# The output projection in token layout: attention output stationary, weights moving in 512 columns

## The chip, the cores and the metric

The kernel runs on one core of a Trainium2 chip. The metric is the device time of one execution in microseconds; lower is better. Times of several executions are given by their median.

## The reference

One layer of an encoder block with 256 tokens and model width 2048, all in float32. What surrounds the change:

```python
mixed = jnp.concatenate([out_a, out_b], axis=-1)   # (1, 256, 2048), the heads' outputs
x = x + mixed @ w_o[l]                             # w_o (2048, 2048): the output projection
h = rms_norm(x, norm_ffn[l])                       # over the 2048 features of a token
x = x + conv_gated_ffn(h, w_up[l], conv_w[l], conv_b[l], w_down[l])   # w_up (2048, 11264), w_down (5632, 2048)
return rms_norm(x, norm_final)
```

Below, y stands for `x + mixed @ w_o`, the residual stream after the projection.

## The kernel before

**Exact float32 by three products.** Every weight tile and every activation is split into a high part (type fp32r) and a low part, the rest. A product is three matmuls into the same PSUM bank: high by high, high by low, low by high (`mm3`, L1002). For each weight tile of 128 x 1024 numbers (512 KB), SP issues the load into a ring of four slots (`raw`), ScalarE writes the high part (`split_hi`, L423), VectorE the low part (`split_lo`, L659), and TensorE multiplies. ScalarE may split tile t once TensorE is through with tile t-4 (`mm_done`), SP may load tile t once the low part of tile t-4 is made (`lo_done`). ScalarE and VectorE run three tiles ahead (`LEAD`). Each engine has one order of work, written out by hand with counting semaphores; nothing is reordered by a planner.

**Stages.** Input projection and attention go in four groups of heads, the attention of one group being laid into the gaps between the tiles of the next. The attention of the last group is laid between the first seven tiles of the output projection (`SLOTS_TAIL`: T transposes probabilities, S makes scores, V multiplies with the values). Then comes the output projection, then the up projection in 22 steps of eight tiles, then the down projection in 88 tiles.

**The output projection before** has 8 units of 256 output features, each of 4 tiles; a tile covers 512 rows of w_o by 256 columns. In `features` (L1008) the weights are stationary and the attention output is moving, in 256 columns (all tokens): 4 row blocks x 2 feature blocks x 3 products = 24 matmuls a tile, 768 in all. The result comes out in feature layout (features on partitions). x, however, lies in token layout in `nat`. So for every unit GpSimd copies 256 columns of x to `xcols` (L403, L406), TensorE transposes them (`turn_x`, L1153, 4 transposes), ScalarE copies them out of PSUM to `xts` (L542), VectorE adds (`make_y`, L831), ScalarE squares (L549) and writes the high part of y times its gain (L551), VectorE adds the squares to `ysum` (L837) and writes the low part (L840). For the later residual y must be in `nat` in token layout as well: TensorE transposes it back (`turn_y`, L1164, 4 transposes) and ScalarE writes it to `nat` (`take_ynat`, L557). The first three units are interleaved by `WOA_ORDER`, units 3 to 7 follow one by one, 4 to 7 in a loop of two passes.

**The second norm's factor** is found behind the first tiles of the up projection: two float32 matmuls with a matrix of ones sum `ysum` over the features and spread the sum over the partitions (L1233), ScalarE takes the root (L594, with a table load), VectorE the reciprocal of 128 x 256 numbers (L878, `r2b`). `r2b` is first used when the first four up tiles are evacuated (L890).

**In the up projection** `up_step` (PE) waits in its first step for the low parts of y that each tile multiplies with; the weights are stationary there, and matmuls of 512 and of 256 columns alternate (L1222, L1224). **In the down projection** (`down`) the activations are stationary and the weights move in 512 columns: 2 row blocks x 2 token blocks x 3 products = 12 matmuls a tile, through the same `mm3`. The result is in token layout and is added to `nat` in place.

Of the kernel before, what the change touches and what calls it, by code (L numbers as in the profile page):

```python
# [5 lines left out]
F32 = mybir.dt.float32  # L25
# [37 lines left out]
T_WOA = T_QUAD + QUADS * QUAD_TILES  # L63
WOA_UNITS = 3
T_WOB = T_WOA + 4 * WOA_UNITS
WO_UNITS = 8
T_UP = T_WOB + 4 * (WO_UNITS - WOA_UNITS)
# [65 lines left out]
def program(nc, x, norm_mix, w_in, sinks, b_f, w_o, norm_ffn, w_up, conv_w, conv_b, w_down, norm_final,  # L133
            ident_c, tri_c, mask_a_c, mask_b_c, cos_c, sin_c, out):
    ctx = ExitStack()
    with ctx:
# [6 lines left out]
        def sem(name):  # L143
# [86 lines left out]
        x_banks = [acc[0][:], acc[2][:], acc[1][:], sc_ps[:, 0], sc_ps[:, 1], tr_ps[:, 0], tr_ps[:, 1], pv_ps[:]]  # L230

# [23 lines left out]
        xcols_s, xt_ps, xts_s, yt_s, ysq_s, yhi_s, ylo_s, yt_ps, ynat_s, ysum_s, y2_ps, y2_root, r2_s = (sem(n) for n in (  # L255
            "xcols_s", "xt_ps", "xts_s", "yt_s", "ysq_s", "yhi_s", "ylo_s", "yt_ps", "ynat_s", "ysum_s", "y2_ps",
            "y2_root", "r2_s"))
# [8 lines left out]
        wo = w_o[0].rearrange("(t c p) n -> t p c n", p=P, c=4)  # L266
# [24 lines left out]
        r3 = small[:, 20:22]  # L291
        g1 = cst[:, 0:KB]
# [10 lines left out]
        def _(sp):  # L303
# [62 lines left out]
        def _(pool):  # L366
# [45 lines left out]
        def _(act):  # L412
# [124 lines left out]
            def take_xt(u):  # L537

                act.wait_ge(xt_ps, u + 1)
                if not (isinstance(u, int) and u == 0):  # L540
                    act.wait_ge(yt_s, u)
                act.activation(xts[:].rearrange("p a n -> p (a n)"), sc_ps[:, 0], ACT.Copy).then_inc(xts_s, 1)  # L542

            def after_y(u, par):

                act.wait_ge(yt_s, u + 1)
                if not (isinstance(u, int) and u == 0):
                    act.wait_ge(ysum_s, u)
                act.activation(ysq[:], yt[:, par], ACT.Square).then_inc(ysq_s, 1)  # L549
                for b in range(2):  # L550
                    act.activation(act_hi[:, bass.ds(u * 2 + b, 1), :].rearrange("p a n -> p (a n)"), yt[:, par, b],  # L551
                                   ACT.Copy, scale=cst[:, bass.ds(u * 2 + (KB + b), 1)]).then_inc(yhi_s, 1)

            def take_ynat(u):

                act.wait_ge(yt_ps, u + 1)
                act.activation(nat[:, :, bass.ds(u * 256, 256)], sc_ps[:, 1].rearrange("p (m n) -> p m n", m=2),  # L557
                               ACT.Copy).then_inc(ynat_s, 1)

            for s in range(4 * WOA_UNITS):  # L560
                split_hi(T_WOA + s + LEAD, (s + LEAD) % RING)
                attention(s, SLOTS_TAIL, QUADS - 1)
                if s in WOA_Y:
                    take_ynat(WOA_Y.index(s))
                if s in WOA_END:
                    after_y(WOA_END.index(s), WOA_END.index(s) % 2)
                if s in WOA_X:
                    take_xt(WOA_X.index(s))

            def wo_unit(u, par):  # L570
                t = u * 4 + (T_WOB - 4 * WOA_UNITS)
                for s in range(4):
                    split_hi(t + (s + LEAD), (s + LEAD) % RING)
                    if s == 0:
                        take_ynat(u - 1)
                    if s == 2:
                        take_xt(u)
                    if s == 3:
                        after_y(u, par)

            wo_unit(WOA_UNITS, WOA_UNITS % 2)
            with act.Fori(0, 2) as i:
                wo_unit(i * 2 + 4, 0)
                wo_unit(i * 2 + 5, 1)
# [725 lines left out]
```

## Time and profile before

| | |
|---|---|
| median of 3 executions | 1118.66 us (1117.6 to 1120.81) |
| span of the profiled execution, first to last instruction | 1116.6 us |
| TensorE matmul busy | 1106.6 us, 99% of the span |
| VectorE busy | 735.4 us, 66% |
| ScalarE busy | 595.8 us, 53% |
| GpSimd busy | 20.9 us, 2% |
| mean granted TensorE clock | 0.998 |
| HBM traffic over the span | 180 GB/s |

The profile gives the profiled execution by its span alone; the median of the timed runs is 2.1 us longer, and that is taken as what lies around the span.

Matmuls are pipelined, so the duration of one in the profile is longer than the time from it to the next: a matmul of 256 columns has 0.28 us, and one starts every 0.12 us. Where time is counted here it goes by starts, or by the number of matmuls in a window of known length. In the chain of waits a group such as "x4" is already in such time. "PE" is matmuls, "PEld" weight loads.

### The profile page before, as it was taken

The page shows a single profiled execution, that of the slowest core. Times are in us where ns is not written, and L with a number is a line of the kernel's source. Part 1 is how long each engine was busy: PE and PEld are TensorE (multiplying, and loading weights), DVE is VectorE, ACT ScalarE, POOL GpSimd, SP SyncE. Part 2 cuts the span into 40 slices and gives each one's busy share as a digit, 9 for nine tenths or more (in the row PEclk, how much of TensorE's full clock was granted, in tenths as well). Part 3 has the DMA queues.
Part 4 walks back from the last instruction along what each step waited for, and adds up shares of the span by engine and source line. Part 5 has one row for each costly group of instructions (what it writes and reads, how often), then busy time and mean ns, then how long its engine had stood idle before and what let it go on. Part 6 is the DMA issues. An engine that isn't in the chain of part 4 may idle for free.

```text
span 1116.6 us, 19616 instructions
## 1 busy us (share of the span) xinstructions
PE 1106.6 (99%) x6873; PEld 978.1 (88%) x6873; DVE 735.4 (66%) x1126; ACT 595.8 (53%) x910; POOL 20.9 (2%) x42
## 2 busy tenths in 40 slices
PE   9999999999999999999999999999999999999997
PEld 8999999999999888888888888888888888888885
DVE  5576767677565677777777777777777545454443
ACT  6846555655555655555555555555555434343432
POOL 1100000000000000000000000000000000000000
PEclk9999999999999999999999999999999999999999
DMA  9674444444455555665566556665555655555553
GB/s 283 188 247 151 152 147 152 138 158 138 144 172 176 178 179 174 202 188 181 169 198 191 182 169 201 190 191 170 184 192 193 229 187 191 187 189 189 187 190 104
DMA packets 178133, 201.90 MB, mean 181 GB/s; under 512 B 8596, under 2 KB 152820, under 8 KB 177968
## 3 DMA queue, kind: packets, MB, share of 16 engines
q1 hardware_dynamic: 176800, 197.69, 55.5%
q0 software_dynamic: 976, 3.37, 0.9%
q8 instruction: 25, 0.41, 0.1%
q10 hardware_dynamic: 320, 0.34, 0.1%
q14 instruction: 12, 0.10, 0.0%
HBM read 199.25 MB, written 2.11 MB: 180 GB/s over the span
## 4 chain that ended last, share of the span: by engine, by line
PE 96%; DVE 2%; ACT 1%; DMA 1%; SPq 0%; issue 0%; DVEq 0%
PE acc L1222 15%; PE tr_ps L1222 15%; PE acc L1004 9%; PE acc L1005 8%; PE acc L1006 8%; PE tr_ps L1224 7%; PE acc L1224 7%; PE sc_ps L1005 4%; PE tr_ps L1005 4%; PE sc_ps L1006 4%; PE tr_ps L1006 4%; PE tr_ps L1004 4%; PE sc_ps L1004 4%; PE sc_ps L1078 1%; PE tr_ps L1085 1%; PE pv_ps L1096 1%
## 5 line engine op out<-in xcount | busy, mean ns | idle before, releaser
L659 DVE TENSOR_TENSOR lo<-raw,hi 128x1024 fp32r<-128x1024 f32 (+1 forms) x368 | 446.6, 1224 | 245.6 <-ACT hi L423 245.1
L423 ACT ACTIVATE hi<-raw 128x1024 fp32r<-128x1024 f32 (+1 forms) x368 | 386.5, 1058 | 201.8 <-PE sc_ps L1006 64.2
L1222 PE MATMUL tr_ps<-act_split,hi 128*128 128x512 f32 x704 | 250.0, 399 | 0.0
L1222 PE MATMUL acc<-act_split,hi 128*128 128x512 f32 x704 | 249.8, 399 | 0.0
L1224 PE MATMUL acc<-act_split,lo 128*128 128x256 f32 x704 | 197.7, 281 | 0.0
L1224 PE MATMUL tr_ps<-act_split,lo 128*128 128x256 f32 x704 | 197.7, 281 | 0.0
L1222 PEld LDWEIGHTS acc<-act_split,hi 128*128 128x128 f32 x704 | 132.3, 188 | 33.0
L1222 PEld LDWEIGHTS tr_ps<-act_split,hi 128*128 128x128 f32 x704 | 132.3, 188 | 32.8
L1224 PEld LDWEIGHTS tr_ps<-act_split,lo 128*128 128x128 f32 x704 | 133.0, 189 | 0.0
L1224 PEld LDWEIGHTS acc<-act_split,lo 128*128 128x128 f32 x704 | 133.0, 189 | 0.0
L1004 PE MATMUL acc<-act_split,hi 128*128 128x256 f32 x416 | 120.1, 289 | 0.0
L1005 PE MATMUL acc<-act_split,hi 128*128 128x256 f32 x416 | 117.6, 283 | 0.0
L1006 PE MATMUL acc<-act_split,lo 128*128 128x256 f32 x416 | 117.5, 282 | 0.0
L1004 PEld LDWEIGHTS acc<-act_split,hi 128*128 128x128 f32 x416 | 79.5, 191 | 3.5 <-issue 3.5
L1005 PEld LDWEIGHTS acc<-act_split,hi 128*128 128x128 f32 x416 | 79.6, 191 | 0.0
L1006 PEld LDWEIGHTS acc<-act_split,lo 128*128 128x128 f32 x416 | 79.6, 191 | 0.0
L1004 PE MATMUL acc<-mix_hi,hi 128*128 128x256 f32 x256 | 74.0, 289 | 0.0
L1006 PE MATMUL acc<-mix_hi,lo 128*128 128x256 f32 x256 | 72.4, 283 | 0.0
L1005 PE MATMUL acc<-mix_lo,hi 128*128 128x256 f32 x256 | 72.2, 282 | 0.0
L1006 PE MATMUL tr_ps<-hi,g_lo 128*128 128x512 f32 x176 | 69.5, 395 | 0.0
L1004 PE MATMUL sc_ps<-hi,g_hi 128*128 128x512 f32 x176 | 69.4, 395 | 0.0
L1005 PE MATMUL sc_ps<-lo,g_hi 128*128 128x512 f32 x176 | 69.4, 395 | 0.0
(187 smaller groups left out, 1473.5 us busy)
## 6 DMA issues: line engine op xcount, KB each, us to landing
raw<-w_up SPq DMA_DIRECT2D x176, 512.0 KB, 4.3
raw<-w_down SPq DMA_DIRECT2D x88, 512.0 KB, 4.3
raw<-w_in SPq DMA_DIRECT2D x72, 512.0 KB, 3.5
raw<-w_o SPq DMA_DIRECT2D x32, 512.0 KB, 3.3
nat<-x SPq DMA_DIRECT2D x8, 256.0 KB, 6.3
key_bias<-nft_dram POOLq DMA_DIRECT2D x4, 512.0 KB, 9.5
result<-nat SPq DMA_DIRECT2D x7, 256.0 KB, 3.0
gfin<-norm_final POOLq DMA_DIRECT2D x1, 1024.0 KB, 7.2
```

The costliest lines, as they stand in the source:

```text
L423: act.activation(hi[:, slot, 0:n], raw[:, slot, 0:n], ACT.Copy).then_inc(hi_done, 1)
L659: dve.tensor_tensor(lo[:, slot, 0:n], raw[:, slot, 0:n], hi[:, slot, 0:n].bitcast(F32), ALU.subtract).then_inc(lo_done, 1)
L1004: pe.matmul(dst, a_hi, b_hi, start=start, stop=False, skip_group_check=True)
L1005: pe.matmul(dst, a_hi, b_lo, start=False, stop=False, skip_group_check=True)
L1006: return pe.matmul(dst, a_lo, b_hi, start=False, stop=True, skip_group_check=True)
L1078: ins = pe.matmul(sc_ps[:, h, c0:c1], qv[:, qs:qs + 128], kv[:, 0:n], start=c0 == 0, stop=True, skip_group_check=True)
L1085: ins = pe.transpose(tr_ps[:, h, c * P:(c + 1) * P], prob[:, p, h, c * P:(c + 1) * P], ident[:])
L1096: pe.matmul(pv_ps[half, 0:S], v[:, 0], prob_t[:, p % 2, h, 0:S], start=True, stop=False, skip_group_check=True)
L1222: pe.matmul(up_banks[v][b].rearrange("p (a n) -> p a n", a=2), wh[:, c, b * P:(b + 1) * P], act_split[:, :, k, :], start=k == 0, stop=Fals ...
L1224: ins = pe.matmul(up_banks[v][b][:, 0:S], wl[:, c, b * P:(b + 1) * P], act_hi[:, k], start=False, stop=True, skip_group_check=True)
```

## The change

The output projection is done in the down projection's manner. It has 4 groups of 512 output features, each of 8 tiles; a tile covers 256 rows of w_o by 512 columns. The attention output (`mix_hi`, `mix_lo`) is stationary and the weights move in 512 columns: 12 matmuls a tile, 384 in all, two PSUM banks a group (one for each half of the tokens). The order of tiles (`WO_ORDER`) interleaves groups 0 and 1 around the last two heads' attention. VectorE adds each bank to x in `nat` in place (`make_y`), after the last tile of the group (`WO_LAST`). ScalarE squares 512 columns with a sum along the row (`y_squares`). One tile later TensorE transposes the 4 x 2 blocks of y (`turn_y`, 8 transposes), ScalarE and VectorE write high and low part from PSUM (`y_hi`, `y_lo`). x is not transposed any more, nor is y transposed back, and GpSimd's copies go. For the norm VectorE sums the 4 partial sums of each token, ScalarE takes the root of 128 x 2 numbers, VectorE the reciprocal and two scaled identity matrices (`diag2`); TensorE multiplies these with ones after the third up tile, and ScalarE copies the result to `r2b`.

The diff, cut to its core (of the removed code, what the section on the kernel before doesn't describe is shown; removed bodies of functions are left out):

```diff
-T_WOA = T_QUAD + QUADS * QUAD_TILES
-WOA_UNITS = 3
-T_WOB = T_WOA + 4 * WOA_UNITS
-WO_UNITS = 8
-T_UP = T_WOB + 4 * (WO_UNITS - WOA_UNITS)
+T_WO = T_QUAD + QUADS * QUAD_TILES
+PAIRS = KB // 2
+T_UP = T_WO + GROUPS * PAIRS
...
-WOA_ORDER = [(0, 0), (1, 0), (2, 0), (0, 2), (1, 2), (2, 2), (0, 1), (1, 1), (0, 3), (2, 1), (1, 3), (2, 3)]
-WOA_END = [8, 10, 11]
-WOA_X = [7, 9, 10]
-WOA_Y = [9, 11]
+WO_ORDER = [(0, 0), (0, 1), (0, 2), (0, 4), (0, 5), (0, 6), (1, 0), (1, 1), (0, 3), (0, 7),
+            (1, 2), (1, 4), (1, 5), (1, 6), (1, 3), (1, 7)] + [(n, p) for n in (2, 3) for p in range(PAIRS)]
+WO_LAST = [max(s for s, (g, _) in enumerate(WO_ORDER) if g == n) for n in range(GROUPS)]
+WO_FIRST = [min(s for s, (g, _) in enumerate(WO_ORDER) if g == n) for n in range(GROUPS)]
...
-        xts = sb("xts", [P, 2, S])
-        yt = sb("yt", [P, 2, 2, S])
-        ysq = sb("ysq", [P, 2, S])
-        ysum = sb("ysum", [P, 2, S])
-        xcols = sb("xcols", [P, MT, 2 * P])
-        assert max(top, sbuf.cursor) <= nc.sbuf_usable_end
+        ysq = sb("ysq", [P, MT, 512])
+        sbuf.cursor = top
+        diag2 = sb("diag2", [P, MT, P])
...
+        wo_banks = [(acc[0][:], acc[2][:]), (acc[1][:], sc_ps[:, 0])]
+        yt_banks = (sc_ps[:, 1], pv_ps[:])
...
-        wo = w_o[0].rearrange("(t c p) n -> t p c n", p=P, c=4)
+        wo = w_o[0].rearrange("(t c p) n -> t p c n", p=P, c=2)
...
-            for n, (u, kt) in enumerate(WOA_ORDER):
-                load(T_WOA + n, n % RING, narrow(raw, n % RING), wo[kt][:, :, u * 256:(u + 1) * 256])
-            with sp.Fori(0, WO_UNITS - WOA_UNITS) as u:
-                load_unit(u * 4 + T_WOB, wo, u * 256 + WOA_UNITS * 256)
+            for s, (n, pair) in enumerate(WO_ORDER):
+                load(T_WO + s, s % RING, wide(raw, s % RING), wo[pair][:, :, n * 512:(n + 1) * 512])
...
-            pool.wait_ge(read_s, 4 * QUADS + 1)
-            pool.tensor_copy(xcols[:], nat[:, :, 0:2 * P]).then_inc(xcols_s, 1)
-            with pool.Fori(1, WO_UNITS) as u:
-                pool.wait_ge(xt_ps, u)
-                pool.tensor_copy(xcols[:], nat[:, :, bass.ds(u * 2 * P, 2 * P)]).then_inc(xcols_s, 1)
...
+            def y_squares(n):
+                if n > 0:
+                    act.wait_ge(ysq_s, MT * n)
+                for m in range(MT):
+                    act.wait_ge(y_s, 2 * n + m + 1)
+                    act.activation(ysq[:, m], nat[:, m, n * 512:(n + 1) * 512], ACT.Square,
+                                   accum_out=ss2[:, m, n:n + 1]).then_inc(ysq_s, 1)
+            def y_hi(n):
+                for b in range(4):
+                    k = 4 * n + b
+                    if b % 2 == 0:
+                        act.wait_ge(yt_ps, 2 * n + b // 2 + 1)
+                    act.activation(act_hi[:, k], yt_banks[b // 2][:, (b % 2) * S:(b % 2 + 1) * S], ACT.Copy,
+                                   scale=g2[:, k:k + 1]).then_inc(yhi_s, 1)
+            for s, (n, pair) in enumerate(WO_ORDER):
+                split_hi(T_WO + s + LEAD, (s + LEAD) % RING)
                 attention(s, SLOTS_TAIL, QUADS - 1)
...
+                if s in WO_LAST:
+                    y_squares(WO_LAST.index(s))
+                if s - 1 in WO_LAST:
+                    y_hi(WO_LAST.index(s - 1))
...
-                        take_ynat(WO_UNITS - 1)
-                    if first and s == 2:
-                        act.wait_ge(y2_ps, 1)
-                        act.activation(ysq[:, 0], pv_ps[:, 0:S], ACT.Sqrt, bias=eps, scale=1.0 / D).then_inc(y2_root, 1)
+                        y_hi(GROUPS - 1)
+                    if first and s == 1:
+                        act.wait_ge(y2_tot, 1)
+                        act.activation(root2, tot2, ACT.Sqrt, bias=eps, scale=1.0 / D).then_inc(y2_root, 1)
+                    if first and s == 3:
+                        act.wait_ge(r2_ps, 1)
+                        act.activation(r2b[:], acc[0][:, 0:S], ACT.Copy).then_inc(r2b_s, 1)
...
+            def make_y(n):
+                for m in range(MT):
+                    cols = nat[:, m, n * 512:(n + 1) * 512]
+                    dve.tensor_tensor(cols, wo_banks[n % 2][m], cols, ALU.add).then_inc(y_s, 1)
+            def y_lo(n):
+                for b in range(4):
+                    k = 4 * n + b
+                    if b % 2 == 0:
+                        dve.wait_ge(yhi_s, 4 * n + b + 2)
+                    dve.scalar_tensor_tensor(act_lo[:, k], yt_banks[b // 2][:, (b % 2) * S:(b % 2 + 1) * S],
+                                             g2[:, k:k + 1], act_hi[:, k].bitcast(F32), ALU.mult,
+                                             ALU.subtract).then_inc(ylo_s, 1)
+            for s, (n, pair) in enumerate(WO_ORDER):
+                split_lo(T_WO + s + LEAD, (s + LEAD) % RING)
                 attention(s, SLOTS_TAIL, QUADS - 1)
...
+                if s in WO_LAST:
+                    dve.wait_ge(mm_done, T_WO + s + 1)
+                    make_y(n)
+                if s - 1 in WO_LAST:
+                    y_lo(WO_LAST.index(s - 1))
...
-                    if first and s == 2:
-                        dve.wait_ge(y2_root, 1)
-                        dve.reciprocal(r2b[:], ysq[:, 0]).then_inc(r2_s, 1)
-                        dve.wait_ge(r2_s, 1)
+                    if first and s == 0:
+                        y_lo(GROUPS - 1)
+                        dve.wait_ge(ysq_s, MT * GROUPS)
+                        dve.tensor_reduce(tot2, ss2, AX.X, ALU.add).then_inc(y2_tot, 1)
                     if first and s == 1:
                         st.done(dve.memset(ub[:, :, :, 0:2], 0.0))
                         st.wait()
+                        dve.wait_ge(y2_root, 1)
+                        dve.reciprocal(r2c, root2).then_inc(r2_s, 1)
+                        dve.wait_ge(r2_s, 1)
+                        for m in range(MT):
+                            dve.tensor_scalar(diag2[:, m], ident[:], r2c[:, m:m + 1], None, ALU.mult).then_inc(diag2_s, 1)
                     if s in (3, 7):
                         v = s // 4
                         dve.wait_ge(upr_s, i * 4 + (2 * v + 2))
                         for b in range(2):
                             st.done(dve.tensor_tensor(up_r[:, b], up_r[:, b], up_banks[v][b][:, 0:S], ALU.add))
                         st.wait()
+                        if first and v == 0:
+                            dve.wait_ge(r2b_s, 1)
...
+            def turn_y(n):
+                if n > 0:
+                    pe.wait_ge(ylo_s, 4 * n)
+                for b in range(4):
                     for m in range(MT):
...
+                        pe.wait_ge(y_s, 2 * n + m + 1)
+                        o = (b % 2) * S + m * P
+                        k = 4 * n + b
+                        ins = pe.transpose(yt_banks[b // 2][:, o:o + P], nat[:, m, k * P:(k + 1) * P], ident[:])
+                    if b % 2 == 1:
+                        ins.then_inc(yt_ps, 1)
+            for s, (n, pair) in enumerate(WO_ORDER):
+                if s == WO_FIRST[0]:
                     pe.wait_ge(evac_d, 3 * QUADS + 1)
...
+                if s == WO_FIRST[1]:
                     pe.wait_ge(evac_a, QUADS + 1)
...
+                    pe.wait_ge(read_s, 4 * QUADS + 1)
+                if s in WO_FIRST[2:]:
+                    pe.wait_ge(y_s, 2 * n - 2)
+                if (n, pair) == (0, QUADS - 1):
                     pe.wait_ge(mixlo_s, 4 * (QUADS - 1) + 3)
...
+                if (n, pair) == (0, 2 * QUADS - 1):
                     pe.wait_ge(mixlo_s, 4 * QUADS + 1)
...
+                pe.wait_ge(lo_done, T_WO + s + 1)
+                wh, wl = wide(hi, s % RING), wide(lo, s % RING)
+                for c in range(2):
+                    k = 2 * pair + c
+                    for m in range(MT):
+                        ins = mm3(wo_banks[n % 2][m], mix_hi[:, k, m * P:(m + 1) * P], mix_lo[:, k, m * P:(m + 1) * P],
+                                  wh[:, c], wl[:, c], start=pair == 0 and c == 0)
+                ins.then_inc(mm_done, 1)
                 attention(s, SLOTS_TAIL, QUADS - 1)
...
+                if s - 1 in WO_LAST:
+                    if s - 1 == WO_LAST[0]:
+                        pe.wait_ge(mixlo_s, 4 * QUADS + 1)
+                    turn_y(WO_LAST.index(s - 1))
...
-                            pe.wait_ge(yt_s, WO_UNITS - 1)
+                            if v == 1:
+                                pe.wait_ge(y_s, MT * GROUPS)
                         else:
                             pe.wait_ge(u_s, i * 4 + (2 * v - 2))
                     if first and v == 0:
-                        pe.wait_ge(ylo_s, 2 * kt + 2)
+                        pe.wait_ge(ylo_s, 4 * kt + 4)
 
...
-                        turn_y(WO_UNITS - 1, 1)
-                    if first and s == 1:
-                        pe.wait_ge(ysum_s, WO_UNITS)
-                        for b in range(2):
-                            ins = pe.matmul(pv_ps[:, 0:S], ones[:], ysum[:, b], start=b == 0, stop=b == 1)
-                        ins.then_inc(y2_ps, 1)
+                        turn_y(GROUPS - 1)
+                    if first and s == 2:
+                        for m in range(MT):
+                            pe.wait_ge(diag2_s, m + 1)
+                            ins = pe.matmul(acc[0][:, m * P:(m + 1) * P], ones[:], diag2[:, m], start=True, stop=True)
+                        ins.then_inc(r2_ps, 1)
             up_step(0, True)
             with pe.Fori(1, UP_STEPS) as i:
                 up_step(i, False)
-            pe.wait_ge(ynat_s, WO_UNITS)
```

## Rows read from the trace of the kernel before

**Rows 1.** The page: busy time (share of the span) and instructions of each engine.

```profile
PE 1106.6 (99%) x6873; PEld 978.1 (88%) x6873; DVE 735.4 (66%) x1126; ACT 595.8 (53%) x910; POOL 20.9 (2%) x42
```

**Rows 2.** Windows: stretch, busy us (instructions) of each engine, granted clock, DMA share, GB/s.

```profile
core 0: us, PE busy (x) PEld busy (x) DVE busy (x) ACT busy (x) POOL busy (x), PEclk, DMA share, GB/s
259.50:364.90 105.40, 105.40 (x889) 103.11 (x888) 63.39 (x88) 57.26 (x92) 5.70 (x8) 1.00 0.49 160
864.00:1109.00 245.00, 245.00 (x1055) 198.38 (x1053) 118.88 (x117) 98.67 (x109) 0.55 (x1) 1.00 0.54 184
```

**Rows 3.** Chain of waits, whole span: start us, us, what; transposes and 128-column products.

```profile
15.54 0.87 PE tr_ps L990 x8
...
34.51 0.45 PE sc_ps L1052 x4
...
306.16 0.44 PE sc_ps L1164 x4
312.29 0.44 PE sc_ps L1153 x4
318.49 0.44 PE sc_ps L1164 x4
324.63 0.44 PE sc_ps L1153 x4
...
361.65 0.44 PE sc_ps L1153 x4
...
371.00 0.86 PE pv_ps L1233 x4
```

**Rows 4.** Line L1153, then line L1164: matmuls, with duration, first and last start.

```profile
L1153 PE MATMUL sc_ps<-ident,xcols x32: 271/272/273, 289.5 to 361.8; 128*128 128x128 f32 x32
...
L1164 PE MATMUL sc_ps<-ident,yt x32: 270/272/273, 296.1 to 367.9; 128*128 128x128 f32 x32
```

**Rows 5.** Chain of waits around the step from w_o to w_up.

```profile
364.85 0.12 PE acc L1006
364.97 0.23 PE tr_ps L1222
...
367.75 0.44 PE sc_ps L1164 x4
```

**Rows 6.** Timeline of VectorE around that step: start, us, group, idle before.

```profile
365.16 0.69 DVE L831 TENSOR_TENSOR yt<-acc,xts 128x512 f32<-128x512 f32 x1 [0.24 <-PE acc L1006]
366.61 0.69 DVE L837 TENSOR_TENSOR ysum<-ysum,ysq 128x512 f32<-128x512 f32 x1 [0.76 <-ACT ysq L549]
367.22 0.87 DVE L840 SCALAR_TENSOR_TENSOR act_split<-yt,cst,act_split 128x256 f32 x2
368.31 1.23 DVE L659 TENSOR_TENSOR lo<-raw,hi 128x1024 fp32r<-128x1024 f32 x1 [0.21 <-ACT hi L423]
```

**Rows 7.** Timeline of ScalarE around that step.

```profile
365.89 0.63 ACT L549 ACTIVATE ysq<-yt 128x512 f32<-128x512 f32 x1 [2.22 <-DVE yt L831]
366.43 0.89 ACT L551 ACTIVATE act_split<-yt,cst 128x256 f32 x2
367.23 1.04 ACT L423 ACTIVATE hi<-raw 128x1024 fp32r<-128x1024 f32 x1
...
372.18 1.28 ACT L594 ACT_TABLE_LOAD   x1
373.48 0.47 ACT L594 ACTIVATE ysq<-pv_ps,small 128x256 f32<-128x256 f32 x1
```

**Rows 8.** VectorE at 268 us: reciprocal of few numbers, and four scalings.

```profile
268.64 0.18 DVE L739 RECIPROCAL stat<-stat 128x4 f32<-128x4 f32 x1 [0.81 <-ACT prob L497]
268.85 1.01 DVE L744 TENSOR_SCALAR prob<-prob,stat 128x128 f32<-128x128 f32 x4
```

**Rows 9.** The page: DMA issues of the three weights, KB each, us to landing.

```profile
raw<-w_up SPq DMA_DIRECT2D x176, 512.0 KB, 4.3
raw<-w_down SPq DMA_DIRECT2D x88, 512.0 KB, 4.3
...
raw<-w_o SPq DMA_DIRECT2D x32, 512.0 KB, 3.3
```

**Rows 10.** Waits from 259 to 375 us: who waited for whom, us, times, longest.

```profile
DVE lo L659 <- ACT hi L423: 30.7, 31, 2.9
...
ACT hi L423 <- PE acc L1006: 6.4, 6, 1.3
...
PEld acc L1004 <- issue: 1.2, 5, 0.3
...
PEld acc L1004 <- DVE lo L659: 0.2, 1, 0.2
```

More of the change, by code:

```diff
@@ L291, in program @@
         r3 = small[:, 20:22]
+        ss2 = small[:, 28:36].rearrange("p (m g) -> p m g", m=2)
+        tot2 = small[:, 36:38]
+        root2 = small[:, 38:40]
+        r2c = small[:, 40:42]
         g1 = cst[:, 0:KB]
@@ L824, in _ @@
                 st.end(QUADS)
-            def make_y(u, par, bank):
-                dve.wait_ge(xts_s, u + 1)
-                if not (isinstance(u, int) and u < 2):
-                    dve.wait_ge(yt_ps, u - 1)
-                dve.tensor_tensor(yt[:, par].rearrange("p a n -> p (a n)"), bank[:], xts[:].rearrange("p a n -> p (a n)"),
-                                  ALU.add).then_inc(yt_s, 1)
-                dve.wait_ge(yt_s, u + 1)
-                dve.wait_ge(ysq_s, u + 1)
-                if not (isinstance(u, int) and u == 0):
-                    dve.wait_ge(ysum_s, u)
-                dve.tensor_tensor(ysum[:], ysum[:], ysq[:], ALU.add).then_inc(ysum_s, 1)
-                for b in range(2):
-                    dve.wait_ge(yhi_s, u * 2 + (b + 1))
-                    ins = dve.scalar_tensor_tensor(
-                        act_lo[:, bass.ds(u * 2 + b, 1), :].rearrange("p a n -> p (a n)"), yt[:, par, b],
-                        cst[:, bass.ds(u * 2 + (KB + b), 1)],
-                        act_hi[:, bass.ds(u * 2 + b, 1), :].rearrange("p a n -> p (a n)").bitcast(F32),
-                        ALU.mult, ALU.subtract)
-                ins.then_inc(ylo_s, 1)
@@ L847, in _ @@
-            for s in range(4 * WOA_UNITS):
-                split_lo(T_WOA + s + LEAD, (s + LEAD) % RING)
-                attention(s, SLOTS_TAIL, QUADS - 1)
-                if s == WOA_END[0] - 1:
-                    st.done(dve.memset(ysum[:], 0.0))
-                    st.wait()
-                if s in WOA_END:
-                    u = WOA_END.index(s)
-                    dve.wait_ge(mm_done, T_WOA + s + 1)
-                    make_y(u, u % 2, acc[u])
-            def wo_unit(u, par, bank):
-                t = u * 4 + (T_WOB - 4 * WOA_UNITS)
-                for s in range(4):
-                    split_lo(t + (s + LEAD), (s + LEAD) % RING)
-                dve.wait_ge(mm_done, t + 4)
-                make_y(u, par, bank)
@@ L1146, in _ @@
                 quad(j, True)
-            def turn_x(u):
-                pe.wait_ge(xcols_s, u + 1)
-                for b in range(2):
+            def turn_y(n):
+                if n > 0:
+                    pe.wait_ge(ylo_s, 4 * n)
+                for b in range(4):
                     for m in range(MT):
-                        ins = pe.transpose(sc_ps[:, 0, b * S + m * P:b * S + (m + 1) * P],
-                                           xcols[:, m, b * P:(b + 1) * P], ident[:])
-                ins.then_inc(xt_ps, 1)
@@ L1157, in turn_y @@
-            def turn_y(u, par):
-                pe.wait_ge(yt_s, u + 1)
-                if not (isinstance(u, int) and u == 0):
-                    pe.wait_ge(ynat_s, u)
-                for m in range(MT):
-                    for b in range(2):
-                        ins = pe.transpose(sc_ps[:, 1, m * S + b * P:m * S + (b + 1) * P],
-                                           yt[:, par, b, m * P:(m + 1) * P], ident[:])
-                ins.then_inc(yt_ps, 1)
-            for s, (u, kt) in enumerate(WOA_ORDER):
-                if s == 0:
+                        pe.wait_ge(y_s, 2 * n + m + 1)
@@ L1187, in _ @@
-                if s in WOA_Y:
-                    turn_y(WOA_Y.index(s), WOA_Y.index(s) % 2)
-            def wo_unit(u, par, bank, free):
-                pe.wait_ge(yt_s, free)
-                for s in range(4):
-                    features(u * 4 + (T_WOB - 4 * WOA_UNITS + s), s, bank, s, mix_hi, mix_lo, s == 0)
-                    if s == 0:
-                        turn_y(u - 1, 1 - par)
-                    if s == 2:
-                        pe.wait_ge(xts_s, u)
-                        turn_x(u)
```

66 lines of the change are left out of this document (3 added, 63 removed).

## The prediction

> **What bounds the kernel now.** I read the page's busy shares first. TensorE multiplies for 1106.6 of 1116.6 us, VectorE works for 66% and ScalarE for 53% [rows 1]. The windows come next: from the first matmul of the output projection to the first of the up projection, and in the down projection, TensorE is busy for the whole window and its granted clock is 1.00, the level of 2.4 GHz [rows 2]. The waits of the stretch say the same from the other side: TensorE waited 0.2 us for a low part and 1.2 us for nothing that shows, while VectorE waited 30.7 us for ScalarE's splits and ScalarE 6.4 us for TensorE [rows 10]. So TensorE sets the pace and the others follow. An instruction taken from TensorE is worth its time from start to start; what is taken from ScalarE, VectorE and GpSimd is worth nothing. The only other thing that can count is a new wait of TensorE.
>
> **The price of the products.** The chain shows a group of transposes at 306.16 and the next at 312.29, with two tiles between [rows 3]. 6.13 less 0.44 for the first group leaves 5.69 us for 48 matmuls of 256 columns: 0.1185 each. The stage's 768 cost 91.0 us. The change puts 384 matmuls of 512 columns in their place. The down projection runs just these: activations stationary, 512 weight columns moving, the same three products, a whole bank as target. 1055 of them take 245.00 us [rows 2], 0.2322 each. 384 cost 89.2 us, so 1.9 us go. The work in columns is the same (196,608 both times); only what each instruction adds to its columns is saved, and that is small. The bounds: at twice 0.1185 a wide matmul would save nothing; at 0.230, the finer reading of single wide starts in the chain (0.23) [rows 5], it would save 2.7. I take the down projection's value, as its instruction stream is the same.
>
> The Trainium skill bears on this, TensorE: Matmul & The Clock Gate, Back-to-back issue gap: an isolated warm matmul takes its columns at 2.4 GHz plus some 2.5 ns. By that, halving the count would save 384 x 2.5 ns, 1.0 us in place of 1.9, and the predicted time would be 0.9 us later. The rows of this kernel show 0.1185 and 0.2322, which lie 12 and 19 ns above the pure column time of 106.7 and 213.3 ns, so the trace does not bear that small addition out; the sum goes by the rows.
>
> **The price of the transposes.** Both directions have 32 transposes before, in groups of four [rows 4]. A group costs the chain 0.44 [rows 3]: 16 x 0.44 = 7.0 us. After the change only y is turned, in four groups of eight. Eight transposes in a row cost 0.87 in the input stage [rows 3]: 4 x 0.87 = 3.5 us. So 3.6 us go. Seven of y's eight groups before, and three of its four after, lie inside the output projection, the last one each behind the first up tile; it makes no difference, since TensorE is the bound in both. I see no reason for a transpose to cost more from `nat` than from `xcols` or `yt`: L990 reads `nat` too. Were a group of eight to cost two switches of the kind of work in place of one, 4 x 0.1 would be added; that is the bound above, and nothing below.
>
> **Loop.** From 312.29 to 324.63 the period of a unit is 12.34 and remains so to 361.65 (three units in 37.02) [rows 3], while twice 6.13 is 12.26. The 0.08 a unit, which units 3 to 7 pay, I put down to how the groups fall and to the loop; in the new order there is neither loop nor four of these groups. 5 x 0.08 = 0.4 us go, with zero as the other end.
>
> **The second norm.** Two float32 products of 256 columns cost 0.86 [rows 3]. Two of 128 columns, the form of the first norm (L1052), cost 0.45 [rows 3]. 0.4 us go.
>
> **The work that stays.** The last heads' attention lies between the tiles as before. Of the window's 105.4 us, 91.0 are products, 15 x 0.44 = 6.6 turns, 0.4 the loop, and 7.4 are left for that attention with its switches and for the window's edges; I carry it over unchanged. Its slots come 0.06 us a tile sooner, since a tile has 12 x 0.2322 = 2.79 us in place of 2.84.
>
> **The new waits of TensorE.** They are what can take the gain back, so each is followed.
> First, the turn of y after the first tile behind each group. A group's last tile ends; VectorE starts its add 0.2 later [rows 5, 6] and needs 0.69 for 512 columns [rows 6], two of them 1.4, so y is ready at about 1.6. TensorE asks for it at 2.79. Cover 1.2 us; behind the waiting transpose are all later tiles. Cost 0. While ScalarE squares (0.63 each) and writes four high parts (0.89 a pair) [rows 7], the next split (1.04) is delayed to about 3.4, its low part (1.23) [rows 6] to about 4.7 after the group's end, and the tile that needs it starts at 3 x 2.79 + 0.87 = 9.2. Cost 0.
> Second, the step to the up projection, zero being its first matmul. ScalarE is through with the squares at 2.5 and with the split of the fourth up tile at 3.5. TensorE ends the first up tile at 2.78 [rows 5] and the turn at 3.65. The high parts follow to 5.3, the low parts (0.87 a pair) to 6.5. The fourth up tile, the first to need them, can start at 3.65 + 2 x 2.78 + 0.45 = 9.7. Cover 3.2 us, cost 0.
> Third, and tightest, the norm's product now stands behind the third up tile and waits for `diag2`. The four sums are reduced on VectorE behind the last low part, at 6.6; ScalarE loads its table for the root, 1.28 [rows 7], to 8.0, and the root of 128 x 2 ends at about 8.3; reciprocal 0.18, start to start 0.2 [rows 8]; two scalings at 0.25 each [rows 8]. With a hand-over of 0.1 to 0.2 at each step `diag2` is ready at 9.0 to 9.4. TensorE comes for it at 3.65 + 5.56 = 9.2. I take 0.2 us of waiting; the ends are 0 and 1.3 (if the chain were a whole table load later). Behind the wait stand the fourth up tile and everything after it. In return the reciprocal of 256 columns goes from VectorE, which is worth nothing by itself. `r2b` is ready 1 us after the product and wanted only when the fourth tile, 2.8 us long, has ended.
>
> **Loads.** A wide tile has 512 KB like the narrow one; at 2.79 us a tile it asks for 188 GB/s, where the stretch now has 160 and the down projection 184 with the DMA engines at 0.54 [rows 2]. Landing took 3.3 us for w_o and 4.3 for w_down [rows 9]. A slot's load is issued when the low part four tiles earlier is made, and is wanted 6.8 us or more later even behind a group's end (low part at 4.7, split at 4 x 2.79 + 0.87 = 12.0 or later). Cost 0, cover at least 2.5 us.
>
> **The sum.** -1.9 - 3.6 - 0.4 - 0.4 + 0.2 = -6.1 us on a span of 1116.6: 1110.5. The median of the timed runs is 2.1 us over the span; I carry that over: 1118.66 - 6.1 = 1112.6 us, 0.55% faster. The ends of the unknown terms together give 1111.2 (wide products at 0.230, no wait) to 1116.6 (wide products and loop save nothing, turns switch twice, full wait).
>
> **The rivals.**
> Small waits eat half of it (chance 0.13). If VectorE comes to the adds late, by more than the 1.2 us of cover, each of three groups and the step to the up projection lose the excess. For it speaks that adds, squares, splits and low parts hand over from engine to engine at one point, and that the third wait has no cover by my count; against it, that VectorE now idles 30.7 us in this stretch [rows 10]. With 0.5 us at four places and 1.3 at the norm's product, 1112.4 + 3.3 = 1115.7. That may still be called no change.
> Loads become the bound (0.04; the other side). If wide tiles of w_o arrived no faster than the stretch's present 160 GB/s [rows 2], a tile would take 524,288 B / 160 GB/s = 3.28 us in place of 2.79 and 32 tiles would add 15.7 us: 1128. It decides at 3.0 us a tile, where the gain is gone (6.1 / 32 = 0.19 over 2.79), a rate of 176 GB/s. Against it: the present 160 is what TensorE asked for, not what the queue could give, and the down projection holds 184 with the same tile shape for 245 us.
> The wide product is cheaper or dearer than in the down projection (0.03 each way, within the ends above): were each matmul's weight load, 0.19 us long by the profile's model, fully hidden at 512 columns and not at 256, the rows of the down projection would already show it. TensorE's weight loads are busy for 103 of 105 us in this stage and 198 of 245 in the other [rows 2], so if anything is hidden better, it is in 0.2322 already.
>
> **How the numbers follow.** The forecast with its own range, 1110.9 to 1114.6, has 0.80; small waits 0.13; loads 0.04; the rest 0.03, split. The range that should hold 8 in 10 is 1110.3 to 1115.8: below by the cheaper product and a median that can fall 1 us either way (the three runs lie between 1117.6 and 1120.8), above to the rival of small waits. A measurement of this kernel can tell about 0.3%, 3.4 us, from no change; faster than that, under 1115.3, has 0.85, within it 0.11, slower 0.04.
>
> **What would show it.** In the profile after: matmuls of 512 columns with `mix_hi` stationary, 128 times each of three products, at 0.232 from start to start; the stretch from the first of them to the first of the up projection at about 99 us (89.2 + 3 x 0.87 + 7.4) in place of 105.4; turns as x8 in four places at 0.87; no x transposes, GpSimd idle there; everything behind the first up step is shifted by one constant. A wait of TensorE for `diag2` of 0 to 0.5 us, none for the adds. The prediction is wrong if the wide products start more than 0.237 apart, if TensorE waits at the group ends, or if the loads of w_o release ScalarE's splits.

## The result and the profile after

The changed kernel takes 1103.8 us (median of 4 executions, 1102.74 to 1104.85), the kernel before 1118.45 beside it: ratio 0.9865, 95% interval 0.985 to 0.9881. I had forecast 1112.6 and a range that ended at 1110.3. The direction was right; the gain is 14.65 us where I had 6.1.

Windows of the kernel after, cut at the first matmul of the output projection, of the up projection and of the down projection, columns as in [rows 2]:

```profile
core 0: us, PE busy (x) PEld busy (x) DVE busy (x) ACT busy (x) POOL busy (x), PEclk, DMA share, GB/s
261.40:360.50 99.10, 99.10 (x469) 79.04 (x468) 56.18 (x77) 48.83 (x80) 0.00 (x0) 1.00 0.53 169
360.50:849.90 489.40, 489.40 (x2829) 431.59 (x2828) 376.71 (x615) 283.21 (x424) 0.00 (x0) 1.00 0.61 188
849.90:1095.00 245.10, 245.10 (x1057) 198.74 (x1056) 118.89 (x117) 98.78 (x109) 0.55 (x1) 1.00 0.57 184
```

The same cuts in the kernel before:

```profile
259.50:364.80 105.30, 105.30 (x888) 103.01 (x887) 63.29 (x88) 57.26 (x92) 5.70 (x8) 1.00 0.49 160
364.80:863.50 498.70, 498.70 (x2826) 432.64 (x2825) 377.34 (x611) 284.99 (x419) 0.00 (x0) 1.00 0.59 185
863.50:1108.90 245.40, 245.40 (x1058) 198.80 (x1056) 118.88 (x117) 98.92 (x109) 0.55 (x1) 1.00 0.54 184
```

The output projection, the stage that was changed, gives 6.2 us, as forecast (99.1 for "about 99"). The up projection, whose 2,816 matmuls are the same, gives 9.3 us more. The forecast had nothing there but the norm's product (0.4 us less) and four more transposes (0.4 us more). TensorE is busy for the whole stage in both kernels and waits for nobody. The down projection has the same length. The spans differ by 13.6 and not 15.5, since the profiled execution after lost 1.9 us at its start to the clock (granted 0.77 of full speed in the first 15 us; the one before had 1.00):

```profile
0.00:15.00 15.00, 11.21 (x56) 10.55 (x57) 4.81 (x13) 6.46 (x12) 4.27 (x12) 0.77 0.88 262
```

Where the 9.3 us are can be seen in starts. First the timeline of TensorE in the kernel before, then in the kernel after, near 600 us; columns: start, modelled duration, group.

```profile
599.25 0.40 PE L1222 MATMUL tr_ps<-act_split,hi 128*128 128x512 f32 x1
599.49 0.28 PE L1224 MATMUL tr_ps<-act_split,lo 128*128 128x256 f32 x1
...
600.66 0.40 PE L1222 MATMUL tr_ps<-act_split,hi 128*128 128x512 f32 x1
```

```profile
599.29 0.39 PE L1147 MATMUL acc<-act_split,hi 128*128 128x512 f32 x1
599.52 0.28 PE L1149 MATMUL acc<-act_split,lo 128*128 128x256 f32 x1
...
600.68 0.39 PE L1147 MATMUL acc<-act_split,hi 128*128 128x512 f32 x1
```

Four pairs of a 512- and a 256-column matmul take 1.41 us before and 1.39 after. At the trace's full resolution, which is a nanosecond, the starts before repeat 240, 120, 236, 114, 232, 118 ns, 353.3 a pair; after they repeat 230, 117, 346.7 a pair. That holds from the second tile of the first step to the last tile: 22.61 and 22.19 us for each of 21 steps. The difference is 6.67 ns a pair (1,060 and 1,040 ns for three pairs); over the 1,400 pairs from the second tile on it makes 9.3 us, of which the first tile, where it is the other way round, takes back 0.05. Below these are called the slow and the quick rhythm.

The rows of the first up step show when each begins. Chain of waits, kernel after:

```profile
360.62 0.23 PE tr_ps L1147
...
363.43 0.44 PE sc_ps L1099 x4
363.87 0.44 PE pv_ps L1099 x4
...
369.85 0.44 PE acc L1158 x4
```

The first tile, from 360.62 to 363.43, takes 2.81 us: slow. Behind the eight transposes the stream is quick, and stays so behind the norm's product. In the kernel before it is the other way round: the first tile is quick, 2.78 us [rows 5], and behind the four transposes at 367.75 it is slow, and stays so.

### The profile page after: what moved, and what is told of

Its sections match the earlier page's. It is cut to its first block, busy times and chain, and to the rows that moved or that the text cites. A ratio compares the mean times of both kernels' runs of the same rounds, so it can differ in the third digit from the quotient of the medians.

```text
span 1103.0 us, 18512 instructions
## 1 busy us (share of the span) xinstructions
PE 1091.7 (99%) x6457; PEld 954.0 (86%) x6457; DVE 727.7 (66%) x1120; ACT 585.3 (53%) x903; POOL 15.1 (1%) x34
## 4 chain that ended last, share of the span: by engine, by line
PE 98%; DMA 1%; SPq 0%; DVE 0%; ACT 0%; issue 0%; DVEq 0%
PE tr_ps L1147 15%; PE acc L1147 15%; PE acc L946 9%; PE acc L947 8%; PE acc L948 8%; PE acc L1149 8%; PE tr_ps L1149 8%; PE sc_ps L948 4%; PE sc_ps L947 4%; PE sc_ps L946 4%; PE tr_ps L947 4%; PE tr_ps L948 4%; PE tr_ps L946 4%; PE sc_ps L1020 1%; PE tr_ps L1027 1%; PE pv_ps L1038 1%
## 5 line engine op out<-in xcount | busy, mean ns | idle before, releaser
L1147 PE MATMUL tr_ps<-act_split,hi 128*128 128x512 f32 x704 | 245.3, 391 | 0.0
L1147 PE MATMUL acc<-act_split,hi 128*128 128x512 f32 x704 | 245.0, 391 | 0.0
L948 PE MATMUL sc_ps<-hi,g_lo 128*128 128x512 f32 x176 | 69.5, 395 | 0.0
L947 PE MATMUL tr_ps<-lo,g_hi 128*128 128x512 f32 x176 | 69.5, 395 | 0.0
L946 PE MATMUL tr_ps<-hi,g_hi 128*128 128x512 f32 x176 | 69.4, 395 | 0.0
```

What stands on the lines that cost most here:

```text
L946: pe.matmul(dst, a_hi, b_hi, start=start, stop=False, skip_group_check=True)
L947: pe.matmul(dst, a_hi, b_lo, start=False, stop=False, skip_group_check=True)
L948: return pe.matmul(dst, a_lo, b_hi, start=False, stop=True, skip_group_check=True)
L1147: pe.matmul(up_banks[v][b].rearrange("p (a n) -> p a n", a=2), wh[:, c, b * P:(b + 1) * P], act_split[:, :, k, :], start=k == 0, stop=Fals ...
```

## The experiments

Theory P: the rhythm is a state of TensorE's stream. Whatever breaks the stream (other work, or a wait) may turn it from one rhythm to the other, nothing else does, and the change altered what stands in the first up step (eight transposes for four, a smaller product one tile later). Rival M: the change relieved the up stage of something (memory traffic, another engine's work, the loop's code).

**Scans.** On TensorE steps 1 to 12 of the up projection are written out in place of the loop, with idle work (its result is not used) behind the first tile of some. The same is done in both kernels:

```diff
+                    if dummy is not None and s == 0:
+                        kind, count = dummy
+                        for n in range(count):
+                            if kind == "T":
+                                pe.transpose(acc[0][:, 0:P], ident[:], ident[:])
+                            else:
+                                pe.matmul(acc[0][:, 0:kind], ones[:], r2b[:, 0:kind], start=True, stop=True)
```

> The changed kernel with steps 1 to 12 of the up projection written out on TensorE and idle transposes or small products put behind the first tile of steps 2, 3, 4, 5 (1, 2, 3, 4 transposes), 7, 8, 9, 10 (6, 8, 4, 4), 11 (a 256-column float32 product) and 12 (a 128-column one). Steps 1, 6 and 13 to 21 have none. Theory P (TensorE's stream of alternating 512- and 256-column matmuls has two rhythms, 346.7 and 353.3 ns a pair, and keeps the one it has until something else is put between): the rhythm changes at some of the insertions and nowhere else, holds until the next, and the steps without insertion take 22.19 or 22.61 us. Rival M (the change freed something else in this stage: memory traffic, an engine, the loop's code): every pair stays at 346.7 ns but for the insertion itself.

> The same insertions in the kernel before. Theory P: it starts at 353.3 ns a pair and goes to 346.7 at some of the insertions, and holds that until the next. Rival M: all pairs stay at 353.3 ns.

Measured, ns a pair in the tile ahead of the insertion and in the tile behind it, each over six pairs from the tile's third start, at the full resolution of the two traces:

```
step and insertion      in the kernel after     in the kernel before
 2   1 transpose        346.7 -> 353.5          353.3 -> 346.7
 3   2 transposes       353.3 -> 353.5          346.7 -> 346.7
 4   3 transposes       353.3 -> 346.7          346.7 -> 353.5
 5   4 transposes       346.7 -> 353.5          353.3 -> 353.5
 6   none               353.3 -> 353.3          353.3 -> 353.2
 7   6 transposes       353.3 -> 346.7          353.3 -> 346.7
 8   8 transposes       346.7 -> 346.7          346.7 -> 346.7
 9   4 transposes       346.7 -> 353.5          346.7 -> 353.3
10   4 transposes       353.3 -> 353.5          353.3 -> 353.5
11   256-column product 353.3 -> 347.5          353.3 -> 347.5
12   128-column product 346.7 -> 346.7          346.7 -> 346.7
```

Between insertions it never changes, over tile borders and steps. Both kernels can have both. M is out: the kernel before reaches the quick rhythm with none of the change, and between the steps of one run nothing was altered but the insertion. The times, 1114.01 and 1119.35 in one execution each, say little with ten insertions. In these two runs four transposes end in the slow rhythm (six of six) and six and eight in the quick one (two of two each); one turned it both times, three both times, two neither. This is no rule: see y turned twice, below.

**One transpose, in each kernel**, behind the fifth up tile of the first step:

```diff
+                    if first and s == 4:
+                        pe.transpose(sc_ps[:, 0, 0:P], ident[:], ident[:])
```

> The kernel before with one idle transpose (identity, into a free bank) behind the fifth up tile, and nothing else. Theory P: one transpose turned the rhythm both times that it was tried, so the stream goes from 353.3 to 346.7 ns a pair and holds it for the 1,368 pairs left: 9.1 us less, 0.1 more for the transpose, 1118.5 - 9.0 = 1109.5. Rival M (the quick rhythm needs something else of the change): 1118.6.

> The changed kernel with the same one transpose at the same place. Theory P: the stream goes from 346.7 to 353.3 ns a pair and stays there: 1103.8 + 9.1 + 0.1 = 1113.0, the time that I had forecast for the change. Rival M: 1103.9.

The kernel before went to 1109.6 us (4 executions, beside 1118.84; ratio 0.9914, 0.9893 to 0.9935), the changed kernel to 1113.08 (7 executions, ratio to before 0.9953, 0.9938 to 0.9968): both to a tenth where P had them. Every execution lies on the same side, 1109.2 to 1111.4 and 1112.7 to 1116.4, so the rhythm goes with the kernel and not with the execution. Up stage, first in the kernel before with the transpose, then in the kernel after with it:

```profile
365.30:854.90 489.60, 489.60 (x2826) 428.16 (x2825) 377.06 (x611) 282.32 (x419) 0.00 (x0) 1.00 0.60 188
```

```profile
358.10:856.70 498.60, 498.60 (x2830) 432.69 (x2829) 376.60 (x615) 285.64 (x424) 0.00 (x0) 1.00 0.59 185
```

So 9 us can be had from the kernel before, or taken from the changed one, by one instruction that computes nothing. The gain of the change itself, at equal rhythm, is 1118.8 - 1113.1 = 5.8 us with both slow, 1109.6 - 1103.8 = 5.8 us with both quick. That the two agree to a tenth is chance, as each ratio is known to about 0.2%, 2 us; by the windows of its own stage the change is worth 6.2 us.

**Eight transposes in the kernel before.**

```diff
+                for rep in range(2 if isinstance(u, int) and u == WO_UNITS - 1 else 1):
...
```

> The kernel before with the last group of y transposed twice, so that eight transposes in place of four stand behind the first up tile, as in the changed kernel. It adds 0.44 us. Theory P: if eight leave the stream in the quick rhythm, the up stage takes some 489.5 us in place of 499 and the time is about 1118.5 + 0.4 - 9.3 = 1109.6; if not, 1118.9. Rival M: 1118.9.

1120.19 us (ratio 1.001, 0.9997 to 1.0023), up stage 499.0. My hope of 1109.6 fell, and the trace says why: behind the eight transposes the next tile has 346.7 ns, as in the scan, and behind the two 256-column products of the second norm, one tile later, it has 353.2 and stays there. The last break counts. (The scans' single product of this width had turned slow to quick; one product and two are not the same break, so that is no contradiction.)

**Wide matmuls in halves**, in the changed kernel's output projection:

```diff
+                        for h in (0, 256):
+                            ins = mm3(wo_banks[n % 2][m][:, h:h + 256], mix_hi[:, k, m * P:(m + 1) * P],
+                                      mix_lo[:, k, m * P:(m + 1) * P], wh[:, c, h:h + 256], wl[:, c, h:h + 256],
+                                      start=pair == 0 and c == 0 and h == 0)
```

> The changed kernel with each wide matmul of the output projection done as two of 256 columns into the halves of the bank: 768 in place of 384, all else alike. My term for the width: the stretch from the first of them to the first up matmul grows from 99.1 by 1.9 us to 101.0, total 1105.7. If an additional matmul costs only 2.5 ns: +1.0, 1104.8. By theory P the rhythm behind it may also come out slow, then some 9 us more, 1115.

```profile
258.80:359.80 101.00, 101.00 (x853) 98.69 (x851) 56.32 (x77) 48.86 (x80) 0.00 (x0) 1.00 0.50 167
359.80:858.40 498.60, 498.60 (x2829) 432.65 (x2828) 376.61 (x615) 285.60 (x424) 0.00 (x0) 1.00 0.59 185
```

The stage grew by 1.9 us, my term for the width. The Trainium skill's addition of 2.5 ns for each isolated matmul (TensorE: Matmul & The Clock Gate, Back-to-back issue gap) would have made it 1.0; these matmuls stand in a stream and not alone, and the measurement decides for 1.9. The total was 1114.03 (ratio 0.996, 0.9949 to 0.9971), since this time the norm's product left the up stage slow. The product is the same as in the changed kernel and finds the quick rhythm in both, and yet it ends in different ones, so the kind of break alone does not decide. The starts just ahead of it do differ (232, 118, 231, 112, 233 ns in the changed kernel; 230, 117, 230, 117, 230 here), but that this phase of the stream is what decides is not shown; the next run speaks against it.

**y turned twice** in the first three groups (`for rep in range(2 if n < GROUPS - 1 else 1)` around the transposes).

> The changed kernel with the first three groups of y transposed twice: 24 more transposes in the output projection. My price of 0.87 us for eight: the stretch from the first wide matmul to the first up matmul grows from 99.1 by 2.6 to 101.7. If a run of transposes is dearer behind wide matmuls, more. The up stage keeps its length of 489.4, unless the stream enters it in another phase (then 499).

Windows of both stages; 2.6 us more in the first, 0.1 in the second, total 1106.93 in one execution:

```profile
260.80:362.50 101.70, 101.70 (x493) 81.63 (x492) 56.69 (x77) 48.84 (x80) 0.00 (x0) 1.00 0.49 165
362.50:852.00 489.50, 489.50 (x2829) 428.19 (x2828) 376.52 (x615) 283.25 (x424) 0.00 (x0) 1.00 0.60 188
```

The 0.1 us has its own story. Behind the last eight transposes, in the first up step, the stream was slow here (353.5 ns) and quick in the changed kernel (346.7), though the starts of the tile ahead are the same in both to the nanosecond or one beside it (118, 241, 120, 235, 114, 232). Two tiles later the norm's product turned it quick. So not even break and visible phase together fix the outcome, and eight transposes do not always end quick.

**Streams of one width.** Idle transposes in the changed kernel, at eight places in the input projection of the first group of heads (the "quad" below) and at twelve in the down projection.

> The changed kernel with idle transposes (1, 2, 3, 4, 6, 8 of them) behind tiles of the first quad of the input projection, where all matmuls have 256 columns, and behind tiles of the first two groups of the down projection, where all have 512. Question: are there two rhythms in a stream of one width too? If so, the mean distance of starts behind an insertion changes between two values (118.6 and 120.0 ns for 256 columns, since both occur in the kernel before) and holds; if not, it goes back to one value within a tile.

256 columns in the input projection, activations moving: 119.4 to 120.0 ns in the tile behind an insertion, with every start 120 apart by its end, and 120.0 in a tile that follows undisturbed; one rhythm. 512 columns: two. Behind four transposes, both times, and behind one the first time the starts alternate 238, 229 ns, mean 233.3, in this and the next two tiles; behind two, three, six and eight, and behind one the second time, they run through 233, 231, 231, 229, 230, 232, 241 with small variations, mean 232.4. The kernels have the latter in the down projection, so nothing is to be gained there. This run took 1114.0. Its 74 transposes at 0.11 us each (four in 0.44) are 8.1 of the 10.2 us over the changed kernel; its up stage was quick; the rest I did not split.

**An empty gap.** In the changed kernel, steps 1 to 10 written out on TensorE, with a wait ahead of tile 5 or 6 of some, counted from 0 (`if s == gap: pe.wait_ge(silu_s, i + 1)`).

> The changed kernel with steps 1 to 10 of the up projection written out on TensorE, and in steps 1, 3, 4, 9 a wait ahead of tile 5, in steps 5, 7, 8 a wait ahead of tile 6, on the gate's activation, which ScalarE ends later than that: TensorE stands idle (some 3 us and some 0.5 us) and nothing is put between. Steps 2, 6 and 10 have none. If the rhythm is set by how the stream starts (theory P), an empty gap can turn it like a transpose does: some of the seven turn. Rival W: only work put between (weight loads) turns it, a gap doesn't; then all pairs stay at 346.7 ns.

Timeline of TensorE at step 5, where the wait left 0.4 us:

```profile
507.33 0.28 PE L1151 MATMUL acc<-act_split,lo 128*128 128x256 f32 x1
508.02 0.50 PE L1149 MATMUL acc<-act_split,hi 128*128 128x512 f32 x1 [0.41 <-ACT silu L565]
508.36 0.28 PE L1151 MATMUL acc<-act_split,lo 128*128 128x256 f32 x1
508.47 0.40 PE L1149 MATMUL acc<-act_split,hi 128*128 128x512 f32 x1
508.71 0.28 PE L1151 MATMUL acc<-act_split,lo 128*128 128x256 f32 x1
```

Of the three short gaps, step 5's turned quick to slow (346.7 to 353.3), step 7's left it slow (352.7, then 353.3), step 8's turned it back to 346.7. W is out: nothing need be put between, a restart is enough. Steps 7 and 8 met their gaps with the same starts (120, 235, 114, 232, 118, 241) and left them in different rhythms, once more without a cause that the trace shows.

The four long gaps ended quick, but behind each, where TensorE had stood idle for some 3 us, it ran for a while at the 1.2 GHz level: the granted clock was 0.54 from 480.8 to 484.5 us, with starts of 512 and 256 columns 426 and 214 ns apart.

```profile
481.60 0.63 PE L1149 MATMUL acc<-act_split,hi 128*128 128x512 f32 x1
482.02 0.41 PE L1151 MATMUL acc<-act_split,lo 128*128 128x256 f32 x1
482.24 0.63 PE L1149 MATMUL acc<-act_split,hi 128*128 128x512 f32 x1
```

So these four say nothing of an empty gap at full clock. Total 1130.63 in one execution.

**Another order of the same matmuls** in the changed kernel's up projection: 512, 512, 256, 256.

```diff
                             pe.matmul(up_banks[v][b].rearrange("p (a n) -> p a n", a=2), wh[:, c, b * P:(b + 1) * P],
                                       act_split[:, :, k, :], start=k == 0, stop=False, skip_group_check=True)
+                        for b in range(2):
                             ins = pe.matmul(up_banks[v][b][:, 0:S], wl[:, c, b * P:(b + 1) * P], act_hi[:, k],
```

> The changed kernel with the up projection's four matmuls of a row block in the order 512, 512, 256, 256 columns in place of 512, 256, 512, 256, the same matmuls otherwise. If what matters is what a width costs in a stream of its own (232.2 and 118.6 ns in the output projection of either kernel), a pair takes 350.8 ns and the time is 1103.8 + 1,408 x 0.0041 = 1109.6. If the order sets a rhythm of its own, it may be anywhere between 346.7 (1103.8) and 353.3 (1113), or under the first, and then this kernel is the fastest.

1106.45 us (ratio to before 0.9887, 0.986 to 0.9915), up stage 491.7; by the starts 348.3 ns a pair. Neither price list holds: the widths' own streams would have made 350.8. The order has at least one rhythm of its own, between the two. The changed kernel as it stands remains the fastest that was run.

## Why the prediction was wrong, step by step

- **The bound: right.** TensorE had no wait for another engine in the stretch but 0.5 us for low parts, and everything else followed.
- **Wide products: right.** 232.4 ns on the mean where I had 232.2; 1.9 us, confirmed by the halves.
- **Transposes: right.** Eight cost 0.87 to 0.88, once and doubled.
- **Norm and attention: right in sum.** The stage is 99.1 long and 99.2 was its sum. The norm's product costs 0.44.
- **Loop: right in size, wrong in cause.** In [rows 3] the long unit is not evenly long. From 306.16 and from 318.49, behind a turn of y, 48 products and a turn take 6.13 and 6.14 us; from 312.29, behind a turn of x, 6.20. By starts the products run 118.7 ns apart behind y and, from unit 3 on, 120.0 behind x. 264 of the stage's 768 ran at 120.0, and 264 x 1.33 ns = 0.35 us is nearly all of my 0.4 for "the loop". It was a rhythm too, a first sight of what decided the result.
- **Loads: right to cost nothing.** The stage moved 169 GB/s and TensorE waited for no load. My 188 was the rate within a tile and the 160 beside it a mean over turns and attention, so the two should not have been compared; nor was the 176 GB/s of that rival a fair mark, as 169 came with the full gain of the stage.
- **New waits: right to cover, too high by 0.2.** Behind each of the four groups y was ready 1.3 us before TensorE came to turn it, where I had 1.2. `diag2` was ready at 368.8 and TensorE came for it at 369.7. The third wait, which I had called tightest and given 0.2 us, had 0.9 us of cover. I had let the table load begin behind the sums (6.6 us into the up projection); it began at 366.44, 6.0 us in, beside the reduction and not behind it. The chain of the fourth group can be followed here (VectorE, then ScalarE):

```profile
360.65 0.69 DVE L786 TENSOR_TENSOR nat<-acc,nat 128x512 f32<-128x512 f32 x1 [0.42 <-PE sc_ps L948]
...
366.47 0.15 DVE L816 TENSOR_REDUCE small<-small 128x2 f32<-128x8 f32 x1
...
368.34 0.48 DVE L824 TENSOR_SCALAR diag<-ident,small 128x128 f32<-128x128 f32 x2
```

```profile
366.44 1.28 ACT L547 ACT_TABLE_LOAD   x1
367.74 0.30 ACT L547 ACTIVATE small<-small 128x2 f32<-128x2 f32 x1
```

- **What failed** is the sentence that "everything behind the first up step is shifted by one constant". I took a stage with unchanged instructions for a stage of unchanged length, and so put the up projection's spacing at no change without a reason. It went from 353.3 to 346.7 ns a pair and gave 9.3 us, more than everything the change took away. With the term at its measured size the sum is 1112.6 - 9.3 = 1103.3, for 1103.8. None of my rivals had it: all of them looked for a stall or for a price, none for the spacing of a saturated stream.
- The ends that I gave for the unknown terms, 1111.2 and 1116.6, don't add up either: the parts named make 1111.6 (0.8 and 0.2 below 1112.6) and 1116.4 (1.9, 0.4, 0.4 and 1.1 above). The result lies below either lower end.
- The trace of before held the hint. The first up tile took 2.78 us [rows 5], and I used that number. The stage is 498.7 us for 176 tiles, 2.83 each with its insertions taken off. One tile in the same stage ran 2% quicker than the 175 behind it, with transposes between. Asking why, there or at the 6.13 and 6.20 us of [rows 3], would have given a rival at 1112.6 - 9.3.

**What stays open.** The runs show that in the up projection the state exists, that it changed at breaks of the stream and nowhere else, that it then holds for 480 us, and that the kind of break does not decide the outcome, nor does the kind of break together with the spacing ahead of it. They don't show what does decide it (so why the change, of all edits, came out quick is luck as far as is known), nor which mechanism of TensorE keeps it. The Trainium skill says (TensorE: Matmul & The Clock Gate, Back-to-back issue gap) that in a stream of weight loads and matmuls the spacing is set by both, pipelined with each other. Several stable alignments of the two would fit what was seen, but no run here separates loads from matmuls, and that is argued, not shown. I also can't predict the outcome of a given break, as the eight transposes showed.

## What to carry to other kernels

Where TensorE is saturated, divide each stage's length by its matmuls and compare with the best stretch of the same instructions, in the trace of before already: a difference of 1 to 2% at full granted clock and with no wait may be a rhythm, and is worth its share of the stage. One idle instruction behind an early tile tests it. When a change alters what stands ahead of a long uniform stream, look at that stream's spacing before the gain or loss is put down to the change; here one idle transpose moves 9 us either way, and the change's own worth is about 6. A setting found this way is fragile: any later edit ahead of the loop may turn it.

## What the runs showed of the hardware

- A stream of alternating 512- and 256-column matmuls on this TensorE has two lasting rhythms, 346.7 and 353.3 ns a pair at full granted clock; a stream of 512 columns has two, 232.4 and 233.3; of 256 columns in the input projection one, 120.0, and in the output projection before two, 118.7 behind a group of y and 120.0 behind a group of x from unit 3 on.
- A break of 0.3 to 0.4 us without work turned it two times in three.
- The same break, met with the same starts ahead of it, left the alternating stream in different rhythms: eight transposes in the changed kernel (346.7) and with y turned twice (353.5), the gaps of steps 7 (353.3) and 8 (346.7).
- Within one kernel the outcome was the same in all timed executions (1109.2 to 1111.4 us for the kernel before with one transpose, 1112.7 to 1116.4 for the changed kernel with it).
- The same four matmuls in the order 512, 512, 256, 256 take 697 ns for two pairs; in the order 512, 256, 512, 256 they take 693 or 707.
